# Delta rules: 64x64 products in the four quarters of the array, layouts that change with each product, and the identity added on the way out of PSUM

## What is computed

```
g = cumsum(g)                                   # within the chunk
decay = exp(where(i >= j, g[i] - g[j], -inf))
lower = where(i > j, (k * beta) @ k.T * decay, 0)
rhs = concat([v * beta, k * beta * exp(g)])
u, w = split(triangular_solve(eye + lower, rhs))     # (I + lower)^-1 @ rhs, one 64x64 system per head and chunk
attn = (q @ k.T) * decay
for each chunk:                                 # S is the state, 128 x 256 per head
    v_new = u - w @ S
    o = (q * exp(g)) @ S + attn @ v_new
    S = S * exp(g_last) + (k * exp(g_last - g)).T @ v_new
```

## Time and profile before

| | us |
|---|---|
| median of 3 runs | 2207.55 (2207.32 to 2212.09) |
| the profiled execution | 2204.82 |
| its span, first to last instruction | 2202.9 |
| PE busy | 2123.0 (96%) |
| DVE busy | 1094.2 (50%) |
| ACT busy | 820.5 (37%) |
| granted TensorE clock, mean | 0.984 |

### The profile page before, as it was taken

The page is one execution under the profiler, slowest core; times in us unless marked ns, Lnnn a source line. Parts: engine busy times, 40 slices in busy tenths (PEclk is TensorE's granted clock), DMA queues, the critical chain, the costliest instruction groups (busy, mean ns, idle before and its releaser), DMA issues. The chain is left out here.

```text
span 2202.9 us, 32326 instructions
## 1 busy us (share of the span) xinstructions
PE 2123.0 (96%) x13672; PEld 1701.6 (77%) x13672; DVE 1094.2 (50%) x1658; ACT 820.5 (37%) x1324; POOL 66.0 (3%) x69
## 2 busy tenths in 40 slices
PE   8989999999999899999999999999998899999999
PEld 6757678888888898667789976669796678888887
DVE  4444765777733366344355644444436544444422
ACT  4324554444422373222433532226435433222211
POOL 0011320000000000000000000000000000000000
PEclk9999999999999999999999999999999999999999
DMA  4331002323233321111224211103220233322232
GB/s 170 106 105 48 1 30 86 96 96 96 96 96 96 106 87 58 39 39 41 95 87 127 77 48 42 47 30 115 88 68 1 87 123 96 93 92 93 96 96 95
DMA packets 51423, 175.65 MB, mean 80 GB/s; under 512 B 6480, under 2 KB 10960, under 8 KB 50640
## 3 DMA queue, kind: packets, MB, share of 16 engines
q1 hardware_dynamic: 51280, 173.59, 24.2%
HBM read 164.07 MB, written 8.45 MB: 78 GB/s over the span
## 5 line engine op out<-in xcount | busy, mean ns | idle before, releaser
L280 PE MATMUL ps<-nx_hi,whi 128*128 128x512 f32 (+3 forms) x1696 | 574.3, 339 | 13.1 <-PEq L2185 6.3
L281 PE MATMUL ps<-nx_lo,whi 128*128 128x512 f32 (+3 forms) x1696 | 571.5, 337 | 0.0
L282 PE MATMUL ps<-nx_hi,wlo 128*128 128x512 f32 (+3 forms) x1696 | 570.5, 336 | 0.0
L266 ACT ACTIVATE whi<-raw 128x1024 fp32r<-128x1024 f32 x282 | 297.4, 1055 | 589.3 <-PE ps L282 532.9
L275 DVE TENSOR_TENSOR wlo<-raw,whi 128x1024 fp32r<-128x1024 f32 x282 | 344.5, 1222 | 259.4 <-ACT whi L266 258.9
L280 PEld LDWEIGHTS ps<-nx_hi,whi 128*128 128x128 f32 x1696 | 321.4, 189 | 57.4 <-DVE wlo L275 7.2
L282 PEld LDWEIGHTS ps<-nx_hi,wlo 128*128 128x128 f32 x1696 | 321.5, 190 | 33.6
L281 PEld LDWEIGHTS ps<-nx_lo,whi 128*128 128x128 f32 x1696 | 321.1, 189 | 34.0
L280 PE MATMUL ps<-mixer_out,whi 128*128 128x512 f32 x384 | 153.7, 400 | 5.8 <-PEq L2812 3.8
L282 PE MATMUL ps<-mixer_out,wlo 128*128 128x512 f32 x384 | 152.9, 398 | 0.0
L281 PE MATMUL ps<-mixer_out,whi 128*128 128x512 f32 x384 | 152.8, 398 | 0.0
(11 more groups left out here) (447 smaller groups left out, 2808.8 us busy)
## 6 DMA issues: line engine op xcount, KB each, us to landing
raw<-stream_dram SPq DMA_DIRECT2D x285, 512.0 KB, 3.5
arena<-keys_dram SPq DMA_DIRECT2D x1, 2112.0 KB, 8.5
h_sb<-x_dram SPq DMA_DIRECT2D x4, 512.0 KB, 6.6
mixer_floats<-cmp_w_k_dram SPq DMA_DIRECT2D x8, 256.0 KB, 4.0
mixer_floats<-cmp_w_v_dram SPq DMA_DIRECT2D x8, 256.0 KB, 4.3
h_dram<-h_sb SPq DMA_DIRECT2D x1, 2048.0 KB, 8.3
gate_dram<-arena SPq DMA_DIRECT2D x1, 2048.0 KB, 8.3
keys_dram<-h_sb SPq DMA_DIRECT2D x1, 2048.0 KB, 9.3
```

The lines of the kernel that those rows point to most:

```text
L266: act.activation(K.whi[:, n % HL], K.raw[:, n % RAW], ACT.Copy).then_inc(K.s_hi, 1)
L280: pe.matmul(out, whi, xhi, start=start, stop=False, skip_group_check=skip)
L281: pe.matmul(out, whi, xlo, start=False, stop=False, skip_group_check=skip)
L282: return pe.matmul(out, wlo, xhi, start=False, stop=stop, skip_group_check=skip)
```

## The change

1. **Quarters.** `mult` now issues its eight matmuls `for k, for r, for c`: the operands come from partition half r, the result goes to half c. All four 64x64 quarters of the array take part, two matmuls each. Results of row half r go to bank `banks[r]`, so that a product fills two banks, 128 columns in each (`pair(banks)`), in place of one bank with 256 columns.
2. **Layouts.** A matrix thus changes its place with every product: which half and which column it is in depends on r, c and k. `entry` names the place of an operand. `flip` and the new `same` leave the half as it is (two quarters at a time), the new `turn` transposes with the move.
3. **The identity is added on the way out of PSUM.** DVE makes y2 = I + x^2 and y4 = I + x^4 beside the copies x2 and x4 (y2 and y4 use the buffers of `ug` and `dt`), and the result is a chain of products, r2 = y2·rr, r4 = y4·r2, r8 = (I + x^8)·r4, copied by ACT, ACT and DVE, in place of sums on DVE. The same in the second half: a4 = I + K^2 is made by DVE out of PSUM, and y is a plain copy.
4. **Two more products a step x**: `turn((4, 5), x1)` behind the flip, and `turn((0, 1), rr)` behind K squared; in the meta part one more, of four 16x16 transposes a group. The side matmuls, their table and the recurrence stay.

```diff
-                    flip(4, x1).then_inc(z["a_t"], 1)
+                    flip(0, x1).then_inc(z["a_t"], 1)
+                    turn((4, 5), x1).then_inc(z["r_t"], 1)
                     side("a_sb")
                     pe.wait_ge(z["a_sb"], n + 1)
-                    mult(5, x1, a1)
-                    mult(0, a1, x1).then_inc(z["p2"], 1)
+                    mult((0, 1), x1, a1).then_inc(z["a2"], 1)
+                    pe.wait_ge(z["r1"], n + 1)
+                    mult((2, 3), a1, x1).then_inc(z["x2"], 1)
                     side("x2_sb")
                     pe.wait_ge(z["a2_sb"], n + 1)
                     pe.wait_ge(z["x2_sb"], n + 1)
-                    mult(1, x2, a2)
-                    mult(2, a2, x2)
-                    pe.wait_ge(z["r1"], n + 1)
-                    mult(4, x2, rr).then_inc(z["p4"], 1)
+                    mult((4, 5), x2, a2).then_inc(z["a4"], 1)
+                    mult((0, 1), a2, x2).then_inc(z["x4"], 1)
+                    mult((2, 3), y2, rr).then_inc(z["r2"], 1)
                     side("a4_sb")
                     pe.wait_ge(z["a4_sb"], n + 1)
                     pe.wait_ge(z["x4_sb"], n + 1)
-                    mult(5, a4, x4)
-                    mult(0, x4, rr).then_inc(z["p8"], 1)
+                    mult((4, 5), a4, x4).then_inc(z["x8"], 1)
+                    pe.wait_ge(z["r2_sb"], n + 1)
+                    mult((0, 1), y4, x1).then_inc(z["r4"], 1)
                     side("x8_sb")
                     pe.wait_ge(z["x8_sb"], n + 1)
-                    pe.wait_ge(z["r3"], n + 1)
-                    mult(1, a1, rr).then_inc(z["p16"], 1)
+                    pe.wait_ge(z["r4_sb"], n + 1)
+                    mult((2, 3), x2, a2).then_inc(z["r8"], 1)
...
-                def mult(b, lhs, rhs):
-                    for q, p in PAIRS:
-                        mm = pe.matmul(quads(b)[half[p], q], lhs[half[p], q], rhs[half[p], q], start=True, stop=True)
+                def entry(m, r, c, k):
+
+                    return m[half[r], 2 * k + c if m is lw else 2 * c + k]
+
+                def mult(banks, lhs, rhs):
+                    for k in range(2):
+                        for r in range(2):
+                            for c in range(2):
+                                mm = pe.matmul(K.ps[half[c], banks[r], CH * k:CH * k + CH], entry(lhs, r, c, k), entry(rhs, r, c, k),
+                                               start=True, stop=True)
...
-                    mult(2, rr, lw)
-                    mult(4, lw, rr)
-                    flip(5, rr).then_inc(z["k_t"], 1)
+                    mult((4, 5), rr, lw).then_inc(z["k_t"], 1)
+                    mult((0, 1), lw, rr)
+                    same(2, lw, rr).then_inc(z["kt"], 1)
                     side("k_sb")
                     pe.wait_ge(z["k_sb"], x + 1)
                     pe.wait_ge(z["kt_sb"], x + 1)
-                    mult(0, x2, a2).then_inc(z["k2"], 1)
+                    mult((4, 5), x2, a1).then_inc(z["k2"], 1)
+                    turn((0, 1), rr).then_inc(z["rr_t"], 1)
                     side("k2_sb")
                     pe.wait_ge(z["k2_sb"], x + 1)
-                    mult(1, a4, x4).then_inc(z["y_t"], 1)
+                    mult((2, 3), a4, x4).then_inc(z["y_t"], 1)
...
-                    dve.wait_ge(z["a_sb"], n + 1)
-                    dve.scalar_tensor_tensor(v4(rr), v4(a1), -1.0, ident4, ALU.mult, ALU.add).then_inc(z["r1"], 1)
-                    dve.wait_ge(z["p2"], n + 1)
-                    dve.tensor_copy(v4(x2), bank(0)).then_inc(z["x2_sb"], 1)
+                    dve.wait_ge(z["r_t"], n + 1)
+                    dve.tensor_tensor(to(rr), one, of((4, 5)), ALU.subtract).then_inc(z["r1"], 1)
+                    dve.wait_ge(z["x2"], n + 1)
+                    dve.tensor_copy(to(x2), of((2, 3)))
+                    dve.tensor_tensor(to(y2), of((2, 3)), one, ALU.add).then_inc(z["x2_sb"], 1)
                     side("lower", "a_sb")
-                    dve.wait_ge(z["p4"], n + 1)
-                    dve.tensor_tensor(v4(rr), v4(rr), bank(4), ALU.add)
-                    dve.tensor_copy(v4(x4), bank(2)).then_inc(z["x4_sb"], 1)
+                    dve.wait_ge(z["x4"], n + 1)
+                    dve.tensor_copy(to(x4), of((0, 1)))
+                    dve.tensor_tensor(to(y4), of((0, 1)), one, ALU.add).then_inc(z["x4_sb"], 1)
...
+                    act.wait_ge(z["a4"], n + 1)
+                    act.activation(to(a4), of((4, 5)), ACT.Copy).then_inc(z["a4_sb"], 1)
+                    act.wait_ge(z["r2"], n + 1)
+                    act.activation(to(x1), of((2, 3)), ACT.Copy).then_inc(z["r2_sb"], 1)
+                    side("x2_sb")
```

More of the change, by code:

```diff
@@ L2167, in quads, with pair, fours, by_bank @@
             return K.ps[:, b, 0:4 * CH].rearrange("p (q n) -> p q n", q=4)
+        def pair(banks):
+            lo, hi = banks
+            return K.ps[:, lo:hi + 1, 0:2 * CH]
+        def fours(ap):
+            return ap.rearrange("p r (k n) -> p r k n", k=2)
+        def by_bank(m):
+            return m[:].rearrange("p (r k) n -> p r (k n)", r=2)
+        def ones4():
+            return cst(K, "ident_half").unsqueeze(1).unsqueeze(1).to_broadcast([P, 2, 2, CH])
         def meta_bank(b):
@@ L2232, in meta_flip, with meta_turn, turn @@
                     return mm
-                def mult(b, lhs, rhs):
-                    for q, p in PAIRS:
-                        mm = pe.matmul(quads(b)[half[p], q], lhs[half[p], q], rhs[half[p], q], start=True, stop=True)
+                def meta_turn(banks, src):
+                    return meta_flip(banks[0], src)
+                def entry(m, r, c, k):
[6 more added lines that the diff above has]
+                                               start=True, stop=True)
+                    return mm
+                def turn(banks, src):
+                    for k in range(2):
+                        for r in range(2):
+                            for c in range(2):
+                                mm = pe.matmul(K.ps[half[c], banks[r], CH * k:CH * k + CH], entry(src, r, c, k),
+                                               cst(K, "ident")[half[r], half[r]], start=True, stop=True)
                     return mm
@@ L2240, in flip, with same @@
                     for q, p in PAIRS:
-                        mm = pe.matmul(quads(b)[half[p], q], src[half[p], q], cst(K, "ident")[half[p], half[p]], start=True, stop=True)
+                        mm = pe.matmul(quads(b)[half[p], q], entry(src, p, q // 2, q % 2), cst(K, "ident")[half[p], half[p]],
+                                       start=True, stop=True)
+                    return mm
+                def same(b, lhs, rhs):
+                    for q, p in PAIRS:
+                        mm = pe.matmul(quads(b)[half[p], q], entry(lhs, p, q // 2, q % 2), entry(rhs, p, q // 2, q % 2),
+                                       start=True, stop=True)
                     return mm
@@ L2250, in _ @@
                 mm.then_inc(z["kk"], 1)
[L2251 removed]
+                invert(0, meta_mult, meta_flip, meta_turn)
                 for h in H4:
@@ L2276, in _ @@
                     mm.then_inc(z["kk"], 1)
-                    invert(x + 1, mult, flip)
-                    mult(2, rr, lw)
-                    mult(4, lw, rr)
-                    flip(5, rr).then_inc(z["k_t"], 1)
+                    invert(x + 1, mult, flip, turn)
+                    mult((4, 5), rr, lw).then_inc(z["k_t"], 1)
+                    mult((0, 1), lw, rr)
+                    same(2, lw, rr).then_inc(z["kt"], 1)
                     side("k_sb")
@@ L2431, in side, with invert, meta_of, flat_quads @@
                             make_hi(K, act, first + c)
[L2433 to L2439 removed]
+                def invert(n, to, of, single):
+                    act.wait_ge(z["a_t"], n + 1)
+                    act.activation(to(a1), single(0), ACT.Copy).then_inc(z["a_sb"], 1)
+                    side("lower")
+                    act.wait_ge(z["a2"], n + 1)
+                    act.activation(to(a2), of((0, 1)), ACT.Copy).then_inc(z["a2_sb"], 1)
+                    side("a_sb")
+                    act.wait_ge(z["a4"], n + 1)
[3 more added lines that the diff above has]
+                    side("x2_sb")
+                    act.wait_ge(z["r4"], n + 1)
+                    act.activation(to(a2), of((0, 1)), ACT.Copy).then_inc(z["r4_sb"], 1)
+                    side("a4_sb")
+                def meta_of(banks):
+                    return meta_bank(banks[0])
+                def flat_quads(b):
+                    return quads(b).rearrange("p (r k) n -> p r (k n)", r=2)
                 act.wait_ge(z["caps"], 1)
@@ L2443, in _ @@
                 side("ug")
-                invert(0, m4, meta_bank)
+                invert(0, m4, meta_of, meta_bank)
                 act.wait_ge(z["u_meta"], 1)
```

67 lines of the change are left out of this document (37 added, 30 removed).

## The result

The changed kernel takes **2185.28 us** in the median of 4 runs (2183.73 to 2186.5), against 2208.1 (4 runs) for the kernel before beside it: a ratio of 0.9899, 95% interval 0.9884 to 0.9915. That is 22.8 us less (19 to 26). A second measurement on another occasion gave 2185.62 against 2207.01, ratio 0.9896 (0.988 to 0.9913). The forecast was 2188.2, faster.

What follows compares the result with a forecast made beforehand. PE was taken as the bound, its side matmuls covering the copies. Products -20.5, meta part +0.2, chunks on DVE +1.0 give -19.3 us: from 2207.55 to 2188.2, range 2185 to 2192, 8 in 10 up to 2209.

Steps and rivals of the forecast that it cites:

- The price of a product in quarters: Delta-stage products: 14.6 ns a pass, 0.233 us a product against 0.465 before; 20.5 us less in eight steps.
- rival (a): Products in quarters: a pass needs 25 ns wherever it runs, 0.41 us a product; 2208.6 us, no change; chance 0.13.
- rival (b): Product batches: the floor holds but PE's queue fills during the cover, short batches fast; half the gain, about 2198; chance 0.09.
- The reason for the 58 ns: A quarter's pass in the products: 64 columns streamed at about 0.85 ns a column fit the 58 ns.
- The two added products: Two more products in each step, 17 in place of 15: 0.47 us a step, included in the 20.5 us.
- The meta part: Four 16x16 transposes a group, eight in all, at 25.6 ns a pass: +0.2 us.
- Handoffs: Copies out of PSUM between products: two DVE operations done at 0.88 us, under a cover of 1.13; no wait, no cost.
- Rival (c): Copies out of PSUM become the bound, with longer operations out of two banks: about 2.5 us a stage, 2193; chance 0.11.
- The chunks on DVE: Side chunks on DVE ahead of x4, y4 and r8 make PE wait: 0.5 us a stage, +1.0 us in all.
- about 2 us in place of 0.7: Sign in the profile after: PE's waits for DVE at the products total about 2 us, at the chunks, against 0.7 before.
- Rival (d): Quarters that share their rows take turns, a product stays at 0.465 us: slower, 2215.2 us; chance 0.09.
- last sign of being wrong: Delta stages: the forecast counts as wrong if the stages shrink by less than the products.

## Why the prediction was right, and where it was off

- **The bound.** PE was the bound, and what its products gave up came off the kernel: 18.9 us from the stages, of a span 18.2 us shorter.
- **The price of a product in quarters** was put at 0.233 us and is 0.235; a batch of 48 passes was to be about 0.9 us and is 0.93. The row that carried it was L757: four quarters at 27.2 ns a pass with twice the columns. The bound of 25.6 ns, from L2226, was a property of one corner of the array: passes in different parts came 14.7 and, with 32 columns of weights, 7.4 to 11 ns apart. With that rival (a) falls, and rival (b) too, since one, two and three products grow evenly (0.46, 0.69, 0.93 us); its picture of fast short batches and slow long ones came only with half the weights. What the Trainium skill says in "TensorE: Matmul & The Clock Gate", "Wait — 56ns, not 53.3ns?", on a start-to-start of never less than about 25 ns doesn't hold between different quarters: here the measurement decides. Its advice in "TensorEngine Tiling (Array Packing)", Performance Considerations, not to take a tiling factor from a dimension that is small already, does not speak against the change, though rival (a) took it to: the same section names a contract dimension and weight columns of 64 as cases for tiling. It agrees with the run that cut the streams from 64 to 32 columns, where a product went from 0.235 to 0.465 us.
- **The reason for the 58 ns was half right.** The prediction took it as 0.85 ns a column of stream and found 64 columns to fit. The run with half streams shows that at 64 columns of weights the stream isn't the only thing that sets it: 32 columns cost the same. For 64x64 products both readings give the same number, so that the sum was not hurt. That they agree is luck: a product with a shorter stream would have been priced too low.
- **The two added products** cost 0.47 us a step, as the sum had it: on the diagonal twice that was found in the stages. The meta part came about as put: from the start of a stage to the first spread it is 20.0 us, before 19.9, some 0.2 us in both stages.
- **Handoffs.** DVE's operations out of two banks take 0.42 and 0.41 us (L2394, L2395), 0.34 apart, and the cover of four holds. Rival (c) falls: that copies out of PSUM may become the bottleneck, as the Trainium skill has it in "TensorEngine Tiling (Array Packing)", Performance Considerations, did not come true in this kernel.
- **The chunks on DVE** were to cost 1.0 us in both stages. At the place that was worked out PE is 0.1 us late (0.43 against 0.37 ahead of 953.73), with DVE's last operation done at 953.20 + 0.41 = 953.61, when the five side matmuls and the gap end at 952.30 + 1.36 = 953.66; PE's list has one wait of 0.2 us more a stage, for L2405, the copy of r8, where the prediction had seen it. 0.6 to 0.7 us in all: the term had the right places and was a little too large. One of its grounds was misread. The 0.7 us for L2355 in two gaps is 0.35 each, no more than the ordinary gap of 0.37, so that PE lost nothing there before. For the same reason the sign "about 2 us in place of 0.7" can't be read off that view: it now names DVE for 3.0 us in eight gaps, but all gaps ahead of products came to 23.3 us in 64 before and 24.3 in 66 after.
- **Rival (d)**, quarters of the same rows in turn, is refuted by the 0.93 us for 48 passes already, and the run by row halves, the order most open to it, shows 0.98, not 1.6.
- **The sum.** By the stages it is -18.9 us against -19.3 forecast. The medians say -22.8 and -21.4, with intervals that reach to about 19. So the forecast of 2188.2 stood 2.9 us above the median. The profiled execution of before (2204.82) lies 3.3 us below its median of 2208.1, and that of after (2186.5) 1.2 above its own, which is where the pair of profiles and the pair of medians part. No row of a stage holds the 2 to 4 us between them; whether they are more than the scatter of the runs stays open. The prediction's last sign of being wrong, stages that shrink by less than the products, contradicts its own sum, which has 20.5 us off the products and 19.3 off the stages; by its letter it was met.

## What to carry to other kernels

Price a packed product by a row of the same packing, even one with another width or in another stage, and not by the densest stream seen in one corner of the array. Where small products keep PE busy in two quarters of the array, spreading them over four halves their time, and it pays to add products and to give up sums in place to get there, as long as the copies between them stay covered; then deal the matmuls out so that neighbours in the program go to different quarters (here 1.8 us a stage). Going on to eight parts by halving the weights lost 15 us again. Once that is done, look at the waits that were there all along: one side chunk ahead of an operation that PE waits for cost 4 us in two stages, and moving one line took it away.

## What the runs showed that was not expected

- A quarter of 64x64 takes a pass in 58 ns whether 32 or 64 columns are streamed; twice as many matmuls of half the columns therefore doubled the product (0.465 us).
- The order of the matmuls within a batch is worth 0.01 to 0.1 us a batch, the more the longer it is, though the quarters work independently.
- In eight parts of 64x32 a single product with its 32 passes took as long as the 16 passes in quarters, 0.45 us, but three took 1.17 in place of 0.93.
- The same stage of the same kernel differed by 3.1 us with the granted clock: 182.7 us at 0.98 and 179.6 at 1.00, and two neighbouring lines of one comparison can differ by more than a term of the sum. These are the second step of the first and of the second stage in the profile of the changed kernel:

```profile
939.80:981.60 41.80, 41.34 (x468) 27.75 (x469) 18.58 (x41) 9.13 (x18) 1.28 (x1) 0.96 0.16 45
1350.80:1391.10 40.30, 39.80 (x468) 26.68 (x469) 19.24 (x41) 9.13 (x18) 1.29 (x1) 1.00 0.16 48
```

  41.8 us at 0.96 and 40.3 at 1.00, with the same 468 passes. Of the two levels, 1.2 and 2.4 GHz, the second of these steps had the upper one throughout. Before the first of them PE had been idle for 1.87 us, waiting for `ug`; that wait stood there in the second stage as well, where the clock did not fall. So the wait alone doesn't decide it, but over all traces it stands beside 10 of its falls. If the two belong together, which no run shows by itself, the wait costs 1.5 us on top of its 1.9 in those executions.
